# One core: attended outputs weighed from values as stationary high and low parts, with turned outputs stored unsplit and split in the merge

## What is computed

```python
# sparse attention, per block of 128 queries; sel are the best-scored keys
s = einsum('btngd,btknd->btngk', q, k_sel) * HEAD_DIM_A ** -0.5
s = where(sel_ok, s, -inf)
o = einsum('btngk,btknd->btngd', softmax(s), v_sel)
# gated delta rule, per chunk of 64 tokens (16 in a sample)
lower = where(strict, einsum('bhid,bhjd->bhij', k_beta, k) * decay, 0)
sol = triangular_solve(eye + lower, [v * beta, k_beta * exp(gc)])
v_new = sol_u - sol_w @ state
o = (q * exp(gc)) @ state + attn @ v_new
# merge
merged = sigmoid(gate_a) * (oa @ w_branch_a) + sigmoid(gate_b) * (ob @ w_branch_b)
x = x + merged @ w_out
```

## Time and profile before

| | before |
|---|---|
| median of 3 runs | 3000.67 us |
| the profiled execution | 3003.59 us, its span 3001.8 us |
| mean granted clock of TensorE | 0.977 of full speed |
| busy: PE, DVE, ACT, POOL | 2862.3, 1650.2, 848.3, 376.1 us |

### The profile page before, as it was taken

One profiled execution on the slowest core, in us unless ns is written; L12 is line 12 of the kernel. 1 busy time (PEld: TensorE's weight loads), 2 busy tenths in 40 slices (PEclk: granted clock), 3 DMA queues, 4 the chain that ended last, 5 costly groups with the idle time before them and its releaser, 6 DMA issues. The chain is left out here.

```text
span 3001.8 us, 43876 instructions
## 1 busy us (share of the span) xinstructions
PE 2862.3 (95%) x16073; PEld 2683.1 (89%) x16073; DVE 1650.2 (55%) x2958; ACT 848.3 (28%) x1485; POOL 376.1 (13%) x477
## 2 busy tenths in 40 slices
PE   8999999999999999999889789699999999999998
PEld 8999999999989799999878678588799999999997
DVE  5444444444451378899355467467744444444445
ACT  4111111111132344554366334311321111111112
POOL 0000000000010045444220266210000000000000
PEclk9999999999999999999999899799999999999999
DMA  4111111111022122222210323632121111111111
GB/s 148 43 42 42 42 42 42 42 42 42 8 58 47 24 71 72 89 84 96 73 48 22 89 70 105 206 132 83 42 64 42 42 42 42 42 42 42 42 35 64
DMA packets 248861, 183.55 MB, mean 61 GB/s; under 512 B 46329, under 2 KB 230185, under 8 KB 248754
## 3 DMA queue, kind: packets, MB, share of 16 engines
q1 hardware_dynamic: 241602, 153.74, 17.8%
q10 hardware_dynamic: 4752, 18.94, 1.7%
q0 software_dynamic: 2400, 9.44, 0.8%
HBM read 142.37 MB, written 39.65 MB: 61 GB/s over the span
## 5 line engine op out<-in xcount | busy, mean ns | idle before, releaser
L524 DVE TENSOR_TENSOR ffn_prod<-ffn_silu,ffn_p_up 128x384 f32<-128x384 f32 x132 | 73.2, 554 | 758.1 <-ACT ffn_silu L432 758.1
L507 DVE SCALAR_TENSOR_TENSOR x<-ffn_p_down,x 128x512 f32<-128x512 f32 x738 | 474.9, 687 | 1.3 <-PE ffn_p_down L157 1.3
L157 PE MATMUL ffn_p_gate<-ffn_hT_hi,ffn_g_hi 128*128 128x384 f32 x1056 | 355.0, 336 | 2.3 <-DVE ffn_hT_lo L263 2.3
L157 PE MATMUL ffn_p_up<-ffn_hT_hi,ffn_u_hi 128*128 128x384 f32 x1056 | 353.7, 335 | 0.0
L157 PE MATMUL ffn_p_gate<-ffn_hT_hi,ffn_g_lo 128*128 128x384 f32 x1056 | 353.6, 335 | 0.0
L157 PE MATMUL ffn_p_gate<-ffn_hT_lo,ffn_g_hi 128*128 128x384 f32 x1056 | 353.5, 335 | 0.0
L157 PE MATMUL ffn_p_up<-ffn_hT_hi,ffn_u_lo 128*128 128x384 f32 x1056 | 353.1, 334 | 0.0
L157 PE MATMUL ffn_p_up<-ffn_hT_lo,ffn_u_hi 128*128 128x384 f32 x1056 | 352.9, 334 | 0.0
L432 ACT ACTIVATE ffn_silu<-ffn_p_gate 128x384 f32<-128x384 f32 x132 | 65.0, 492 | 859.9 <-PE ffn_p_up L157 859.9
L157 PE MATMUL ffn_p_down<-o_c_hi,o_t_lo 128*128 128x512 f32 x756 | 295.4, 391 | 0.0
L157 PE MATMUL ffn_p_down<-o_c_lo,o_t_hi 128*128 128x512 f32 x756 | 294.9, 390 | 0.0
(11 more groups left out here) (390 smaller groups left out, 5149.4 us busy)
## 6 DMA issues: line engine op xcount, KB each, us to landing
ffn_raw_g<-in_ffn_w_gate SPq DMA_DIRECT2D x44, 512.0 KB, 5.1
ffn_raw_u<-in_ffn_w_up SPq DMA_DIRECT2D x44, 512.0 KB, 6.2
ffn_raw_d<-in_ffn_w_down SPq DMA_DIRECT2D x44, 512.0 KB, 3.7
h_raw<-in_w_in SPq DMA_DIRECT2D x32, 512.0 KB, 3.9
projected_d<-sp_stage ACTq DMA_DIRECT2D x20, 576.0 KB, 2.8
conv_d<-sp_stage ACTq DMA_DIRECT2D x12, 576.0 KB, 3.2
dl_qkv<-conv_d SPq DMA_DIRECT2D x27, 256.0 KB, 4.5
x<-in_x_prompt SPq DMA_DIRECT2D x8, 512.0 KB, 7.1
```

The costliest lines, as they stand in the source:

```text
L157: mm = nc.tensor.matmul(out, stationary(k)[a], moving(k)[b], start=(start and at == 0 and i == 0), stop=(stop and 3 * at + i == n - 1))
L507: nc.vector.scalar_tensor_tensor(out=xs, in0=p_down[(NO * q + o) % 4][:], scalar=0.5, in1=xs, op0=ALU.mult, op1=ALU.add).then_inc(added, 1)
L524: nc.vector.tensor_tensor(prod[:, slot], silu[:, slot], p_up[slot][:, 0:TG], ALU.mult).then_inc(prod_done, 1)
```

## The change

In `attend`, the values are split once into high and low parts that stand side by side as a stationary operand of 128 columns (`v_parts`). The turned probabilities are split as well, ScalarE casting a bank (`turned_hi`) and VectorE subtracting it (`turned_lo`, `keep_rest`), and two units of a pair are the moving side together, 256 columns. Units are ordered so that the four heads of one key group follow one another. The result comes out turned, with 64 rows for the high and 64 for the low part of the values; every four units ScalarE copies one half and VectorE adds the other (`join`). One over the total is put on a diagonal (`put_on_diagonal`) and spread over the rows by a product with ones (`spread_totals`). Turns and splits of finished tiles are gone; outputs are stored once, unsplit. The mask is written where the probabilities will stand.

In `delta`, tile 0 takes GpSimd's block solve too. The direct levels 1 to 3, their masks and `below_first` are gone, both first fronts run ahead of the first solve, and SP's block loads are ordered anew. Only the first three tiles' outputs are split there; the others are stored unsplit. In `merge`, groups 1 and 2 are loaded unsplit and split by ScalarE (`split_high`) and VectorE (`split_rest`); the loads of group 2 wait for the split of group 1. Feed-forward 2 makes the additions of tiles 7 and 8 separately. The core of the diff:

```diff
-ADDS_BEFORE = [(3,), (4, 5), (6,), (7, 8)] + [()] * (NT - 4)
+ADDS_BEFORE = [(3,), (4, 5), (6,), (7,), (8,)] + [()] * (NT - 5)
...
-        units = [(t, j, kv) for t in range(NTP) for j in range(4) for kv in range(KV)] + [
+        units = [(t, j, kv) for t in range(NTP) for kv in range(KV) for j in range(4)] + [
...
+            def weigh(pair, half=None):
...
+                    if k == 0:
+                        pe.wait_ge(turned_rest, before[2 * pair + 2])
...
+                    nc.tensor.matmul(out, v_parts[:, kv, k, :], turned_hi[:, pair % 2, k].rearrange("p h q -> p (h q)"),
+                                     start=(k == 0 and first), stop=False)
+                    mm = nc.tensor.matmul(out, v_parts[:, kv, k, :], turned_lo[:, pair % 2, k].rearrange("p h q -> p (h q)"),
+                                          start=False, stop=(k == n - 1 and not first))
...
+            def spread_totals(g):
...
+                nc.tensor.matmul(p_oT[0:HD].rearrange("p h q -> p (h q)"), const.rest[:, ONES, 0:HD], diag[:, g % 2, :],
...
+            def put_on_diagonal(u):
...
+                nc.vector.tensor_scalar(diag[:, g % 2, j * P:(j + 1) * P], const.ident[:], rtotal[:, j:j + 1], None,
...
+            def keep_rest(u):
...
+                    dve.wait_ge(turned_high, before[u] + i + 1)
...
+                    nc.vector.tensor_tensor(turned_lo[:, pair % 2, ks, u % 2, :], p_pT[(before[u] + i) % 2][:, 0:ks.stop - ks.start, :],
+                                            turned_hi[:, pair % 2, ks, u % 2, :].bitcast(F32), ALU.subtract).then_inc(turned_rest, 1)
...
+            def join(g):
+                dve.wait_ge(low_kept, g + 1)
+                nc.vector.tensor_tensor(out_sum[:], p_o[0:HD, :], out_sum[:], ALU.add).then_inc(joined, 1)
...
+                nc.vector.tensor_tensor(oT[:, g % 2], out_sum[:].rearrange("p (h q) -> p h q", h=4), p_oT[0:HD],
...
-                if u >= 1:
-                    norm(u - 1)
...
+                for g in joined_at(u):
+                    join(g)
+                invert(u)
+                if u < DEC:
+                    put_on_diagonal(u)
...
+                    keep_rest(u)
...
-    return range(1 if n == 0 else BLOCK_LEVEL, LEVELS_P) if n < NTP else range(0)
+    return range(BLOCK_LEVEL, LEVELS_P) if n < NTP else range(0)
...
-            to_blocks(1)
...
+            send_lower(0)
+            to_blocks(0)
+            send_lower(1)
+            from_blocks(0)
+            to_blocks(1)
...
-                if n == NTP - 2:
-                    first.load(sp, a_parts_d, b_parts_d)
+                if n == NTP - 3:
+                    first.load(sp, attended_d)
...
             front(0)
-            for m in range(1, NT):
+            front(1)
+            solve(0)
+            solve(1)
+            for m in range(2, NT):
...
-            load_operands(sp, operands[1], parts_d, slice(TG, 2 * TG), operands_in[1])
-            sp.wait_ge(first.parts_stored, 32 * NT)
-            load_operands(sp, operands[2], parts_d, slice(2 * TG, TOK), operands_in[2])
+            for g in range(1, NG):
+                mine = slice(g * TG, (g + 1) * TG)
+                if g >= 2:
+                    sp.wait_ge(a_rest, g - 1)
+                sp.dma_start(raw_a[:], attended_d[:, :, mine].rearrange("n p t -> p n t")).then_inc(raw_a_in, 16)
+                if g >= 2:
+                    sp.wait_ge(b_rest, 2 * (g - 1))
+                for i in range(2):
+                    sp.dma_start(raw_b[i], gated_d[heads[i], :, mine].rearrange("n p t -> p n t")).then_inc(raw_b_in, 16)
...
+            def split_rest(g):
...
+                nc.vector.tensor_tensor(a_lo[:], raw_a[:], a_hi[:].bitcast(F32), ALU.subtract).then_inc(a_rest, 1)
```

More of the change, by code:

```diff
@@ new lines, in norm_dec @@
+            def norm_dec(u):
+                j = units[u][1]
+                q = slice(u % 4, u % 4 + 1)
+                dve.wait_ge(weighed, 2 * LAST_GROUP + 3 + u - DEC)
+                if j >= 2:
+                    dve.wait_ge(o_turned, j - 1)
+                for half in own:
+                    mul = nc.vector.tensor_scalar(o_dec[half, j % 2, :], p_o[half, half], rtotal[half, q], None,
+                                                  ALU.mult)
+                mul.then_inc(normed, 1)
@@ new lines, in keep_turned, with keep_turned_dec @@
+                if pair >= 2:
+                    act.wait_ge(weighed, pair - 1)
+                for i in range(groups[u]):
+                    act.wait_ge(prob_turned, before[u] + i + 1)
+                    ks = slice(4 * i, min(4 * i + 4, cols(u)[1] // P))
+                    nc.scalar.copy(turned_hi[:, pair % 2, ks, u % 2, :],
+                                   p_pT[(before[u] + i) % 2][:, 0:ks.stop - ks.start, :]).then_inc(turned_high, 1)
+            def keep_turned_dec(u):
+                at, width = cols(u)
+                if u == DEC:
+                    act.wait_ge(tail_stored, 96)
+                if u >= DEC + 2:
+                    act.wait_ge(weighed, 2 * LAST_GROUP + 2 + u - DEC - 1)
+                act.wait_ge(prob_turned, before[u] + 1)
+                bank, full = p_pT[before[u] % 2], width // P
+                nc.scalar.copy(probT[:, u % 2, 0:full * P].rearrange("p (k q) -> p k q", k=full), bank[:, 0:full, :])
+                nc.scalar.copy(probT[0:SEQ_S, u % 2, full * P:(full + 1) * P], bank[0:SEQ_S, full, :]).then_inc(
+                    probT_ready, 1)
@@ L2338, in step @@
                         (hat_q, lower, attend_in_tile)[third](m)
+                    elif n == NTP - 1 and third == 0:
+                        first.keep_rest_a(dve)
                     elif n == NTP - 1 and third == 2:
@@ L2342, in step @@
                         norm_out(n - 3)
-                if n >= 3:
-                    keep_rest(n - 3)
+                    if 3 <= n < 3 + FIRST and third == 2:
+                        keep_rest(n - 3)
                 if n:
@@ L2352, in _ @@
             dve.wait_ge(barred, 2)
-            gaps(0)
-            hat_k(0)
-            hat_q(0)
-            lower(0)
-            attend_in_tile(0)
-            first_y()
+            for m in range(2):
+                gaps(m)
+                hat_k(m)
+                hat_q(m)
+                lower(m)
+                attend_in_tile(m)
+            expand(0, 1)
+            expand(0, 0)
             def spread_values(h):
```

569 lines of the change are left out of this document (277 added, 292 removed).

## The result

The changed kernel takes 3019.74 us in the median of five runs (3015.84 to 3022.18) against 3002.09 for the kernel before in five runs beside it (2998.97 to 3007.16): a ratio of 1.006, 95% interval 1.0043 to 1.0076. The sign and the main mechanism of the prediction hold; the sum was 32.0 us and 17.65 came (16.2 by the spans of the two profiled executions, 3018.0 and 3001.8, at a mean granted clock of 0.979 and 0.977).

What follows compares the result with a forecast made beforehand. TensorE bounds attend's wide tiles before the change; afterwards a closed VectorE-ScalarE loop was to. Terms 21.5 + 2 + 10 + 2 + 7.3 - 3.8 - 6 - 1 = +32.0, with 3003.59 - 2.92, gave 3033 us, range 3008 to 3052.

Steps and rivals of the forecast that it cites:

- Wide tiles: Attend, tiles of 5 to 8 pieces of 128 keys: 21.5 us more over 32 units, plus 2 for joining output halves.
- The loop: Attend, wide tiles: mask, exponential, cast, subtractions, next mask form a closed circle, 4.36 us at 1024 keys, 3.27 at 640.
- Narrow tiles: Attend, narrow tiles, 32 units: VectorE's added work and hand-overs cost 10 us more, ends 0 and 16.
- VectorE's own work fills the slot: Attend, narrow tiles: no loop closes, but VectorE's operations sum to 2.02 us a unit, 64.6 us where 60.9 elapse.
- Delta's start: Start of delta: two GpSimd solves in a row make tile 1 start 7.3 us later, ends 3.3 and 9.
- Later tiles follow at that pace: Delta, after tile 1: later tiles keep their pace, so nothing of the 7.3 us is given back.
- Delta's tail: End of delta: a store wait of 5.79 us goes, a 2.0 us subtraction comes; net -3.8, ends 0 and -5.8.
- Merge: Merge: second group's operands come 3.9 us earlier, the third gains as much or nothing; -6, ends 0 and -7.8.
- Second feed-forward: Second feed-forward: the turn TensorE awaits for 2.56 us stands behind one addition less; -1 us, ends 0 and -2.6.
- The free loop: Rival, attend's wide tiles: exponential and subtraction overlap, the tiles keep 100.6 us, 21.5 less, 3011 us; chance 0.09.
- the TensorE rival: Rival, attend: TensorE still ends the stage, both banks' subtraction takes 0.7 us instead of 1.19; 2981 us, chance 0.09.
- The fallen clock: Rival, attend: half the wide units run at 1.2 GHz because TensorE idles, 18 us more, 3051 us; chance 0.12.

Runs made afterwards that it cites:

- kernel 3: The changed kernel with tiles 7 and 8 added together again in the second feed-forward, as in the kernel before; 3016.94 us, 1.0059 of the kernel before.
- kernel 5: The changed kernel with ScalarE's cast of a tile's outputs ahead of the logarithm again in delta; 3023.54 us, 1.0075 of the kernel before.
- Experiment 1: The changed kernel with ScalarE's casts of a unit ahead of the next unit's exponential in tiles over 512 keys; 2993.39 us, 0.9975 of the kernel before.
- experiment 2: The changed kernel with TensorE making every turn of a wide unit twice; 3021.92 us, 1.0077 of the kernel before.
- experiment 8: Kernel 6 with the diagonal of one over the total made on GpSimd instead of VectorE; 2986.53 us, 0.9953 of the kernel before.
- experiment 4: The kernel before with ScalarE's logarithm ahead of the cast of another tile's outputs in delta, nothing else moved; 2994.29 us, 0.9977 of the kernel before.
- Kernel 9: The changed kernel with the old attend weighing, outputs stored unsplit, and the old order of additions; 2982.18 us, 0.9942 of the kernel before.
- kernel 6: The changed kernel with casts ahead of the next exponential in tiles over 512 keys and the old order of additions; 2990.84 us, 0.9965 of the kernel before.

## Why the prediction came out as it did

**Wide tiles (+21.5, and 2 for the joins): right, by its own steps.** The loop was priced at 4.36 us for 1024 keys; its slots in tile 7 are 4.26 to 4.53, most of them 4.40; at 640 keys it was priced at 3.27, and the last four masks of tile 4 stand (1582.69 - 1572.85) / 3 = 3.28 apart. The sum of the two terms is 23.5 and 25.1 came. The rest lies in the first half of tile 4, where four slots of 3.28 would be 13.1 us and 1572.85 - 1557.91 = 14.94 went by. One slot of 3.88 has six casts of keys and queries for a later tile on ScalarE, ahead of its exponential. One of 4.70, with a join, falls to the lower clock level; with the same attend code it takes 3.66 in kernels 3 and 5 (see the end). Experiment 1 opens the loop and takes 26 us away, experiment 2 shows that TensorE does not set it. The hand-over of 0.04, which no row had shown, is not to be seen in the row after the change: the cast at 1655.33 begins as the exponential ends.

**Narrow tiles (+10): right in size (8.3), half right in reason.** The sum took one mean width for all of them. VectorE is the busiest engine in tiles 2 and 3 only, and these have 6.7 of the 8.3 us. The diagonal costs 0.29 us in the row at 1654.25, with the next one free to start 0.2 later (1523.47, then 1523.67 for the subtraction), where 0.28 stood in the sum. The step "VectorE's own work fills the slot" is borne out in part in tile 3: experiment 8 takes 2.1 us of VectorE's busy time away there (18.40 to 16.26), and the tile becomes 1.1 shorter. How the rest divides between hand-overs, taken as 6.4 of the 10, and the clock of tile 2, which falls from 1.00 to 0.90 with the change, no run shows. The Trainium skill's rule (VectorE: DVE Perf Modes, "The perf-mode tier table (the rule you actually need)") is that such an operation runs at twice the rate of a two-source one; its times are for 2048 columns. At 128 columns the trace shows no such gain: the diagonal takes 0.29 us, and the two-source subtraction of 128x128 from PSUM 0.28. So the estimate of 2 us that the rule would have taken off this term is near the 1.7 by which the term was too large, but by chance as far as the trace shows.

**Delta's start (+7.3): the size was wrong.** The first solve came as forecast: 24.1 us after the stage's start, and 24.7 was worked out. The step that failed is the 4.0 us from a solve's end to its packed load, taken from the earlier trace rows. GpSimd's last copy ends and SP goes on at once (GpSimd, then SP's queue, then GpSimd again, in the changed kernel):

```profile
1748.23 0.60 POOL L2597 COPY dl_turned<-dl_solved 32x256 f32<-32x256 f32 x1
```

```profile
1750.79 0.93 SPq L1968 DMA_DIRECT2D dl_packed<-solved_d  x2
```

```profile
1754.56 0.11 POOL L2590 MEMSET dl_solved<- 32x16 f32 x1 [5.74 <-DMA dl_solved<-lower_d]
```

It takes 2.0 us from the solve's end at 1748.83 to the load. The second solve then starts 5.7 us after the first one's end, where 7.7 was priced, and from the second solve's end to tile 1, where the same 4.0 was part of 5.92, it takes 4.4. So tile 1 starts 55.1 us after the stage's start instead of 52.4: +2.7, a little under the lower end of 3.3, which had been put there for the first of the two.

**Delta's middle: a term that was missing.** "Later tiles follow at that pace, so nothing of it is given back" was the wrong step. The pace itself changed, from 20.9 to 19.5 us, because the diff also turned the order of the logarithm and the cast on ScalarE. I had read the diff of delta for what was removed and added and had not set ScalarE's program before against after. Experiments 4 and 5 show the step in both directions. By tile 8 it has turned +2.7 into -4.8 (197.9 us after the stage's start before, 193.1 after). Of these 7.5 us, experiment 4 finds 5.8 in the kernel before (192.1); the other 1.7 I did not trace.

**Delta's tail (-3.8): right in sign, short.** From tile 8 to the stage's end 42.9 us have become 36.2, -6.7, just past the end of -5.8. VectorE's new subtraction costs less of it than the 2.0 that I set against the store; what covers it I did not trace.

**Merge (-6): right for the second group, wrong for the third.** TensorE's waits in the kernel before, behind that of the earlier trace rows, and then in the changed one:

```profile
1952.85 0.41 PE L157 MATMUL mg_p_a<-mg_a_hi,bw_wa_hi 128*128 128x384 f32 x1 [1.28 <-issue]
...
1973.21 0.41 PE L157 MATMUL mg_p_a<-mg_a_hi,bw_wa_hi 128*128 128x384 f32 x1 [3.85 <-DVE mg_part_b L2777]
```

```profile
1953.36 0.41 PE L156 MATMUL mg_p_a<-mg_a_hi,bw_wa_hi 128*128 128x384 f32 x1 [0.93 <-DVE mg_a_lo L2816]
1956.14 0.41 PE L156 MATMUL mg_p_b<-mg_b_hi,bw_wb_hi 128*128 128x384 f32 x1 [0.46 <-DVE mg_b_lo L2819]
1961.38 0.60 PE L156 MATMUL mg_p_a<-mg_a_hi,bw_wa_hi 128*128 128x384 f32 x1 [2.91 <-DVE mg_a_lo L2816]
...
1983.19 0.66 PE L156 MATMUL mg_p_a<-mg_a_hi,bw_wa_hi 128*128 128x384 f32 x1 [6.08 <-DVE mg_part_b L2838]
```

The second group waits 0.93 and 0.46 (1953.36 and 1956.14) where the earlier trace rows had 6.63: 5.2 less, and 3.9 was priced. The step that failed is the third group's, which was to gain as much or nothing: it waits 2.91 where 1.28 stood (1961.38 and 1952.85), 1.6 more, since its load starts only behind the split of the second group, and its own split follows. Further on the products wait 6.08 for VectorE where 3.85 stood, 2.2 more. VectorE waits there for the split of the next weights, and ScalarE's cast for their load. ScalarE before, and then after:

```profile
1966.02 0.62 ACT L2635 CAST bw_wa_hi<-br_raw_a 128x512 fp32r<-128x512 f32 x1 [2.84 <-DMA br_raw_a<-in_w_branch_a]
```

```profile
1975.27 0.62 ACT L2658 CAST bw_wa_hi<-br_raw_a 128x512 fp32r<-128x512 f32 x1 [4.31 <-DMA br_raw_a<-in_w_branch_a]
```

In both kernels SP issues that load as soon as GpSimd has split the weights before it, and the cast starts 5.2 to 5.3 us behind the issue. The issue comes 5.4 us earlier in the stage than before, and ScalarE reaches the cast 7.0 us earlier. So a part of the gain is lost in this load, which I had not followed; no experiment moved it, so this is a reading of these rows.

**Second feed-forward (-1): wrong in sign, +5.2.** The turn came 1.2 us earlier, as priced; what stands ahead of the separated addition on VectorE, and that TensorE's first product waits for it, was not looked at. The gap of 3.84 us and the slow products behind it make the rest (below).

**The rivals.** The free loop (wide tiles at 100.6) and the TensorE rival (a subtraction of 0.7 us for both banks) fell: the pair takes 1.29 us. The fallen clock was not what set the wide tiles: from 1640 to 1660 TensorE has a gap of some 1.5 us in every slot and a granted clock of 1.00, its 2.4 GHz level. It came in one slot of tile 4, for about 1.0 us, where the rival had 18. The swinging between levels that the Trainium skill (TensorE: Matmul & The Clock Gate, "A second HAM failure mode: psum-queue depth-cycling") reports for short idles is not what this trace shows from 1640 to 1660; the one slot of tile 4 stands at the end.

**What had no term.** The sample units at the end of attend are 3.2 us shorter. Kernel 9, whose attend differs from that of the kernel before only in its unsplit outputs, has 30.9 us there too, against 34.1. So it is the outputs' split and second store that are missing here, and not the new weighing; I had looked at them for the prompt tiles only, and priced them at nothing.

**The balance.** The forecast stood 13 us too high, with errors of both signs: too high were delta (15.0), the stages ahead (4.3), the samples (3.2) and attend's prompt tiles (1.7), too low the feed-forward (6.2) and the merge (2.3), in all 15.7; and the 2.9 taken off for the profiled execution of before were not met by such a difference after, where the profiled execution took the median itself, 3019.74. 15.7 - 2.9 = 12.8, to the rounding of the cuts. So attend is forecast by its mechanism. For delta, merge and feed-forward together -3.5 was forecast and -10.0 came, with two of the three wrong in sign; that their errors offset one another in part is luck.

## What to carry to other kernels

When an added operation goes from engine A to B and back to A, write both engines' programs in their order and add up the circle before anything else: here the order of two steps on ScalarE is worth 26 us with the same work, and the saved products of TensorE nothing while the loop was closed. An operation that waits for another engine should not stand ahead of one that needs nothing from it, a table load and a logarithm above all (1.4 us a tile). When an addition is moved, look up who waits for it and what stands ahead of it now; and a large change that loses should be cut into its stages, since here the losing part hid 17 us of gain in the others.

## What the runs showed of the hardware

**A fast operation on VectorE waits for GpSimd.** Of the 64 diagonals most take 0.29 us; seven take from 0.37 to 0.82, and each of these seven lies over an instruction of GpSimd that had begun before it or with it. The longest, on VectorE, and what GpSimd does then:

```profile
1565.38 0.82 DVE L1575 TENSOR_SCALAR at_diag<-ident,at_rtotal 128x128 f32<-128x128 f32 x1
```

```profile
1564.82 1.29 POOL L1372 TENSOR_TENSOR at_queries<-sa_qkT,at_queries 64x512 fp32r<-64x512 f32 x1 [16.10 <-ACT at_queries L1646]
```

GpSimd ends at 1566.11 and the diagonal at 1566.20; the other six end 0.08 to 0.09 after GpSimd's instruction too. Three others that begin in the last 0.13 us of such an instruction are not longer, and in kernels 1 and 6 one that begins 0.03 to 0.04 us behind the start of one takes 1.32 us. All 64 take 20.8 us, where 64 times 0.286 would be 18.3, so this is 2.5 us of VectorE's time. Not all of it reaches the stage: behind the longest, VectorE's next subtraction waits 1.15 us for ScalarE. The Trainium skill (SBUF — State Buffer, "Who interferes with whom") says that the two engines hold a shared pair of ports exclusively, that a one-source operation in a two-port mode takes it, and that the later one waits for the whole instruction of the other. The trace agrees, 0.82 against 0.29 us. The subtractions and masks, which read PSUM, show no such spread (0.01 us within a shape).

**A gap brings the lower clock in some places and not in others.** After the 3.84 us gap in the second feed-forward TensorE comes back at its 1.2 GHz level. Windows of the changed kernel, over the gap, behind it, and further on:

```profile
2176.00:2181.00 5.00, 1.09 (x8) 0.86 (x8) 3.80 (x7) 3.14 (x6) 0.00 (x0) 0.89 0.16 49
2181.50:2186.50 5.00, 5.00 (x16) 5.00 (x17) 3.75 (x6) 0.20 (x1) 0.00 (x0) 0.50 0.33 98
2187.00:2190.00 3.00, 3.00 (x20) 2.96 (x19) 0.69 (x1) 1.64 (x3) 0.00 (x0) 1.00 0.00 0
```

The granted clock is 0.50 from 2181.5 to 2186.5 and the products of 384 columns take 0.52 us and start 0.32 apart; behind that they take 0.34 and start 0.17 to 0.18 apart. Some 17 products at 0.32 instead of 0.17 are 2.5 us more, so the gap cost over half its length again. With the old order the wait of 2.56 us at the same place is followed by products of 0.34 at once (experiment 3). The gaps of some 1.5 us in the slots from 1640 to 1660 brought no such fall. In the fourth slot of tile 4 it went both ways with the same attend code; the slot in the changed kernel and then in kernel 3:

```profile
1568.15:1572.85 4.70, 4.67 (x17) 2.77 (x18) 3.40 (x10) 1.68 (x4) 1.19 (x3) 0.64 0.00 1
```

```profile
1568.14:1571.80 3.66, 3.06 (x15) 1.87 (x16) 3.33 (x11) 1.68 (x4) 1.19 (x3) 1.00 0.00 0
```

TensorE had been idle ahead of it for 2.04 us in the one and 2.05 in the other. Behind this, the two products that spread the totals take 1.94 us and 1.07, and the slot is 1.04 us longer at the lower level. What tells the two apart these traces don't show.
